# Two-layer hybrid block: low parts of the split weights written over the raw pieces, four slots instead of four and two

## The reference

```python
def first_block(x, ...):
    for layer in range(2):
        x = x + 0.5 * swiglu(rmsnorm(x, ffn1_norm[layer]), ffn1_w_gu[layer], ffn1_w_down[layer])
        h = rmsnorm(x, mix_norm[layer])
        y = mixer_gated_deltanet(h, ...) if layer == 0 else mixer_sliding_window_sinks(h, ...)
        x = x + y
        x = x + 0.5 * swiglu(rmsnorm(x, ffn2_norm[layer]), ffn2_w_gu[layer], ffn2_w_down[layer])
    return rmsnorm(x, final_norm)

def second_block(x, p, ...):                      # hybrid, ffn4 and ple in the kernel's names
    z = rms_norm(x, norm_mix) @ w_in              # q, k, v; RWKV columns; two gates
    attn = windowed_gqa(q, k, v, sink)            # 8 query heads of 64, 2 key heads, T = 256
    rwkv = rwkv7_time_mix(shifted z, ...)         # 8 heads of 64, both directions
    x = x + merged(gates, attn @ w_up_attn, rwkv @ w_up_rwkv) @ w_out
    x = x + squared_relu_ffn(rms_norm(x, ...))    # width 4096
    return x + gated per-layer embedding of p
```

## Time and profile before

| | |
|---|---|
| median of 3 runs | 1692.92 us (1690.53 to 1695.64) |
| the profiled execution | 1697.04 us, span 1695.0 us |
| mean granted TensorE clock | 0.974 of full speed |
| matmuls on PE | 15411 |
| splits of whole pieces on ACT and DVE | 223 each; the two permuted pieces are split in 8 quarters |

### The profile page before, as it was taken

The page is one execution under the profiler, slowest core; times in us unless marked ns, Lnnn a source line. Parts: engine busy times, 40 slices in busy tenths (PEclk is TensorE's granted clock), DMA queues, the critical chain, the costliest instruction groups (busy, mean ns, idle before and its releaser), DMA issues.

```text
span 1695.0 us, 35795 instructions
## 1 busy us (share of the span) xinstructions
PE 1592.7 (94%) x15411; PEld 1527.7 (90%) x15411; DVE 1055.6 (62%) x1274; ACT 730.1 (43%) x811; POOL 74.9 (4%) x53
## 2 busy tenths in 40 slices
PE   7999899878899999999998999999978999999997
PEld 7999899777899999999988999999857778999997
DVE  4765577653666647664677665568666654767345
ACT  5343345532534345433555433454643322555342
POOL 1000000000100001000101000031110000100000
PEclk9999999989999999999999999999979999999998
DMA  8655545000656556555434665554100021555550
GB/s 274 209 187 186 191 134 173 26 2 19 203 177 190 182 186 187 179 192 191 158 101 150 185 192 194 184 183 142 58 2 3 2 101 52 173 176 183 188 191 34
DMA packets 155064, 243.24 MB, mean 144 GB/s; under 512 B 9283, under 2 KB 106174, under 8 KB 154814
## 3 DMA queue, kind: packets, MB, share of 16 engines
q1 hardware_dynamic: 154510, 240.63, 43.6%
q10 hardware_dynamic: 432, 0.79, 0.2%
HBM read 240.34 MB, written 1.05 MB: 142 GB/s over the span
## 4 chain that ended last, share of the span: by engine, by line
PE 83%; DVE 10%; ACT 4%; issue 2%; DMA 0%; SPq 0%; DVEq 0%; ACTq 0%
PE dense_ps L2390 23%; PE dense_ps L2391 22%; PE dense_ps L2392 22%; PE mixer_ps L456 3%; DVE w_lo L2770 2%; PE dense_ps L456 2%; ACT w_hi L2595 1%; PE mixer_ps L1082 1%; PE mixer_ps L1657 1%; DVE qkv L887 1%; PE mixer_ps L1091 1%; DVE xT L2886 1%; ACT ly_r L502 0%; PE mixer_ps L1100 0%; DMA raw<-in_ffn_w_gu 0%
## 5 line engine op out<-in xcount | busy, mean ns | idle before, releaser
L2770 DVE TENSOR_TENSOR w_lo<-raw,w_hi 128x2048 fp32r<-128x2048 f32 x223 | 513.1, 2301 | 377.1 <-ACT w_hi L2595 376.5
L2390 PE MATMUL dense_ps<-h_hi,w_hi 128*128 128x256 f32 x2368 | 669.8, 283 | 24.4 <-DVE h_lo L2845 15.1
L2391 PE MATMUL dense_ps<-h_lo,w_hi 128*128 128x256 f32 x2368 | 663.3, 280 | 0.0
L2392 PE MATMUL dense_ps<-h_hi,w_lo 128*128 128x256 f32 x2368 | 663.3, 280 | 0.0
L2595 ACT ACTIVATE w_hi<-raw 128x2048 fp32r<-128x2048 f32 x223 | 427.6, 1918 | 513.1 <-PE dense_ps L2392 490.6
L2390 PEld LDWEIGHTS dense_ps<-h_hi,w_hi 128*128 128x128 f32 x2368 | 451.0, 190 | 31.6 <-issue 27.3
L2392 PEld LDWEIGHTS dense_ps<-h_hi,w_lo 128*128 128x128 f32 x2368 | 449.3, 190 | 0.0
L2391 PEld LDWEIGHTS dense_ps<-h_lo,w_hi 128*128 128x128 f32 x2368 | 447.7, 189 | 0.7 <-issue 0.5
L2390 PE MATMUL dense_ps<-g_hi,w_hi 128*128 128x256 f32 x960 | 266.5, 278 | 2.8 <-DVE w_lo L2770 2.6
L2392 PE MATMUL dense_ps<-g_hi,w_lo 128*128 128x256 f32 x960 | 266.0, 277 | 0.0
L2391 PE MATMUL dense_ps<-g_lo,w_hi 128*128 128x256 f32 x960 | 266.0, 277 | 0.0
(11 more groups left out here) (526 smaller groups left out, 1858.9 us busy)
## 6 DMA issues: line engine op xcount, KB each, us to landing
raw<-in_ffn_w_gu SPq DMA_DIRECT2D x176, 512.0 KB, 4.7
raw<-in_ffn_w_down SPq DMA_DIRECT2D x88, 512.0 KB, 4.2
raw<-in_w_ff SPq DMA_DIRECT2D x64, 512.0 KB, 4.3
raw<-in_w_in SPq DMA_DIRECT2D x36, 512.0 KB, 4.2
raw<-in_a_w_in SPq DMA_DIRECT2D x32, 512.0 KB, 4.4
raw<-in_a_w_out SPq DMA_DIRECT2D x8, 512.0 KB, 4.1
raw<-in_b_w_in SPq DMA_DIRECT2D x8, 512.0 KB, 4.0
raw<-in_b_w_out SPq DMA_DIRECT2D x8, 512.0 KB, 4.1
```

Of the source, the lines that this page charges most:

```text
L2390: pe.matmul(o, hi, mh, start=start, stop=False)
L2391: pe.matmul(o, hi, ml, start=False, stop=False)
L2392: return pe.matmul(o, lo, mh, start=False, stop=stop)
L2770: dve.tensor_tensor(w_lo[:, p % 2, :], raw[:, p % RAW_SLOTS, :], w_hi[:, p % 2, :].bitcast(F32), ALU.subtract).then_inc(lo_ready, 1)
```

## The change

- **Slots.** There is one number of slots, four, for `w_hi` and for `raw`; `w_lo` has the memory of `raw`, so DVE writes the low part over the raw piece. The load of piece p now waits for `piece_used` of piece p - 4. ACT's split waits for the load alone.
- **Order of splits.** ACT's first split of the next stage stands ahead of its wait for `dense_drained` in `norm`; DVE's is at the end of the down projection (`pieces_of[down] - 1`), and the one in `residual` behind the first half is gone. In mixer_a one split moves into the second inverse (level 3 on ACT, level 5 on DVE) and two follow the last output. In mixer_b the splits at the beginning go, and two stand together at the end (n == 6 on ACT, n == 7 on DVE). In the hybrid's norm two stand where one stood, and out2's last `splits(2)` becomes 3.
- **Hybrid heads.** Query columns are no longer permuted: the pieces of in2 are split like all others. The queries of a key head lie on both partition halves, so the keys are needed on both: a matmul with the constant `swap` writes them to a sixth column block of `qk`. `scores(0)` moves from tile 1 to tile 3, `turned_(0)` from 6 to 7, `values(0)` to tile 1 of chunk 1.
- **Shared space.** mixer_a's second group lies over slot 0 of `w_hi`, slot 0 of `raw` and the end of the arena (`h_lo`); the hybrid's matrices over slots 2 and 3 of `w_hi` and of `raw`. POOL waits for `piece_used` before it fills them.

```diff
-RAW_SLOTS = 4
-SPLIT_SLOTS = 2
+SLOTS = 4
...
-    raw = fixed.take("raw", [P, RAW_SLOTS, PIECE])
-    w_hi = fixed.take("w_hi", [P, SPLIT_SLOTS, PIECE], F32R)
-    w_lo = fixed.take("w_lo", [P, SPLIT_SLOTS, PIECE], F32R)
+    w_hi = fixed.take("w_hi", [P, SLOTS, PIECE], F32R)
+    raw_at = fixed.at
+    raw = fixed.take("raw", [P, SLOTS, PIECE])
+    w_lo = Map(nc, raw_at, fixed.at).take("w_lo", [P, SLOTS, PIECE], F32R)
...
-    HEAD_PIECES = [PIECE_OF["in2"] + i for i in range(2)]
-
-    def by_heads(tensor, slot, k):
-        return tensor[:, slot, 512 * k:512 * k + 512].rearrange("p (s t d) -> p t s d", s=2, t=4)
...
-    SET_A = (group_set(m, 0), group_set(Map(nc, base, base + 3 * PIECE * 4), 1))
...
+    assert (PIECE_OF["a_out"] + 3) % SLOTS == 0
+    SET_A = (group_set((m, m, m), 0),
+             group_set([Map(nc, at_, at_ + PIECE * 4) for at_ in (base, raw_at, arena - PIECE * 4)], 1))
...
+            if lv == 3:
+                splits(1)
...
-        pool.wait_ge(lo_ready, PIECE_OF["a_out"] + 2)
+        pool.wait_ge(piece_used, PIECE_OF["a_out"])
...
+            if lv == 5:
+                splits(1)
...
-        splits(1)
         finished(1)
-        splits(1)
+        splits(2)
...
             if n in (4, 6):
-                splits(1)
-        splits(1)
+                splits(1 + n // 6)
...
             if n in (5, 7):
-                splits(1)
+                splits(1 + n // 7)
...
-    m = Map(nc, base, base + RAW_SLOTS * PIECE * 4)
-    assert PIECE_OF["up_attn"] % RAW_SLOTS == 0
+    m = Map(nc, base + 2 * PIECE * 4, raw_at)
...
-                 "slots": (0, 1, 2, 3), "ot": 2 * s_, "sink": 32 + 4 * s_} for b in range(NB) for s_ in range(2)]
+                 "slots": (0, 2, 1, 3), "ot": 2 * s_, "sink": 32 + 4 * s_} for b in range(NB) for s_ in range(2)]
 
     def q_c(g, t):
-        return qk[64 * g["half"]:64 * g["half"] + 64, t, P * g["blk"]:P * g["blk"] + P]
+        return qk[64 * (t % 2):64 * (t % 2) + 64, 2 * g["half"] + t // 2, P * g["blk"]:P * g["blk"] + P]
 
     def k_c(g, t):
-        return qk[64 * g["half"]:64 * g["half"] + 64, 4, :]
+        return qk[64 * (t % 2):64 * (t % 2) + 64, 4 if t % 2 == g["half"] else 5, :]
...
+            if n == 0 and kt == 1:
+                pe.wait_ge(c_qkv, 1)
+                pe.matmul(M_ps[:, 3, T:2 * T], constant("swap"), qk[:, 4, :], start=True, stop=True).then_inc(c_vturn, 1)
+            if 1 <= n <= 4 and kt == (1 if n == 1 else 0):
+                values(n - 1)
+            if 0 <= n < 4 and kt == (1 if n else 3):
                 if n == 0:
-                    pe.wait_ge(c_qkv, 1)
+                    pe.wait_ge(c_qkv, 2)
                     pe.wait_ge(att_mask, masks_c["at"])
                 scores(n)
-            if 0 <= n < 4 and kt == 6:
+            if 0 <= n < 4 and kt == (6 if n else 7):
                 if n:
                     pe.wait_ge(att_out, base_ + n)
                 turned_(n)
-            if 1 <= n <= 4 and kt == 0:
-                values(n - 1)
...
-        pool.wait_ge(lo_ready, PIECE_OF["up_attn"])
+        pool.wait_ge(piece_used, PIECE_OF["in2"] + 2 * COUNT_OF["in2"])
...
+        dve.wait_ge(c_vturn, 2)
+        dve.tensor_copy(qk[:, 5, :], M_ps[:, 3, T:2 * T]).then_inc(c_qkv, 1)
...
-        splits(2)
+        splits(3)
...
-                slot = p % RAW_SLOTS
-                if p >= RAW_SLOTS:
-                    sp.wait_ge(lo_ready, p - RAW_SLOTS + 1 + RAW_SLOTS * turn)
+                slot = p % SLOTS
+                if p >= SLOTS:
+                    sp.wait_ge(piece_used, p - SLOTS + 1 + SLOTS * turn)
...
-                act.wait_ge(raw_loaded[p % RAW_SLOTS],
-                            32 * (p // RAW_SLOTS + 1 + turn) + (16 if p >= PIECE_OF["b_in"] else 0))
-                if p >= SPLIT_SLOTS:
-                    act.wait_ge(piece_used, p - SPLIT_SLOTS + 1 + 4 * turn)
-                if p in HEAD_PIECES:
-                    assert isinstance(turn, int)
-                    for k in range(4):
-                        last = act.activation(as_heads(w_hi, p % 2, k), by_heads(raw, p % RAW_SLOTS, k), ACT.Copy)
-                    last.then_inc(hi_ready, 1)
-                    return
-                act.activation(w_hi[:, p % 2, :], raw[:, p % RAW_SLOTS, :], ACT.Copy).then_inc(hi_ready, 1)
+                act.wait_ge(raw_loaded[p % SLOTS],
+                            32 * (p // SLOTS + 1 + turn) + (16 if p >= PIECE_OF["b_in"] else 0))
+                act.activation(w_hi[:, p % SLOTS, :], raw[:, p % SLOTS, :], ACT.Copy).then_inc(hi_ready, 1)
...
                 for half in range(2):
+                    if half == 0 and stage in BEFORE:
+                        splits(1)
...
-                    if half == 0 and stage in BEFORE or stage == "ffn0" and half == 0:
+                    if half == 0 and stage == "ffn0":
...
-                    splits(1 if stage in ("mixer_b", "hybrid") else 2)
+                    splits(2)
...
-                dve.tensor_tensor(w_lo[:, p % 2, :], raw[:, p % RAW_SLOTS, :], w_hi[:, p % 2, :].bitcast(F32),
+                dve.tensor_tensor(w_lo[:, p % SLOTS, :], raw[:, p % SLOTS, :], w_hi[:, p % SLOTS, :].bitcast(F32),
...
-                    if e == 0 and ahead_of_split:
-                        splits(1)
...
-                        splits(pieces_of[down] - 2)
-                    residual(down, 1.0 if up == "ff1" else 0.5, s != "ffn0")
+                        splits(pieces_of[down] - 1)
+                    residual(down, 1.0 if up == "ff1" else 0.5)
```

More of the change, by code:

```diff
@@ L272, in alone @@
         eng.nop().then_inc(sem("passed"), 1)
-    raw_loaded = [sem(f"raw_loaded{i}") for i in range(RAW_SLOTS)]
+    raw_loaded = [sem(f"raw_loaded{i}") for i in range(SLOTS)]
     hi_ready = sem("hi_ready")
@@ L386, in build, with group_set @@
     m.at = at
-    def group_set(m_, g):
-        return {n: m_.take(f"{n}{g}", [P, c, P]) for n, c in (
-            ("v_tok", 8), ("neg_lt", 8), ("att_t", 8), ("q_dec", HG), ("k_dec", HG), ("inv", 8), ("inv_t", 8))}
-    SET_A = (group_set(m, 0), group_set(Map(nc, base, base + 3 * PIECE * 4), 1))
+    PARTS = ((("v_tok", 8), ("neg_lt", 8)), (("att_t", 8), ("q_dec", HG), ("k_dec", HG)), (("inv", 8), ("inv_t", 8)))
+    def group_set(maps, g):
+        return {n: m_.take(f"{n}{g}", [P, c, P]) for m_, part in zip(maps, PARTS) for n, c in part}
+    assert (PIECE_OF["a_out"] + 3) % SLOTS == 0
+    SET_A = (group_set((m, m, m), 0),
+             group_set([Map(nc, at_, at_ + PIECE * 4) for at_ in (base, raw_at, arena - PIECE * 4)], 1))
     at = m.at
@@ L1027, in beside_first @@
                 query_norm(1)
-                dve.wait_ge(lo_ready, PIECE_OF["a_out"] + 2)
+                dve.wait_ge(piece_used, PIECE_OF["a_out"])
                 values_kept(1)
@@ L1138, in sink @@
             of_heads = bcast[:, g["sink"]:g["sink"] + 4]
-            if g["slots"][1] == 1:
-                return of_heads.rearrange("p (a b) -> p a b", b=2)
             return of_heads.rearrange("p (a b) -> p b a", b=2)
@@ L1345, in mixer_b_dve @@
             last.then_inc(dense_drained, 1)
-            splits(1)
+            if e:
+                splits(1)
             if "ffn3" in STAGES:
@@ L1366, in build @@
     zp = m.take("zp", [P, ZT, T + 2])
-    qk = m.take("qk", [P, 5, T])
+    qk = m.take("qk", [P, 6, T])
     v_c = m.take("v_c", [P, 1, T])
@@ L1396, in build @@
     ar_raw = m.take("ar_raw", [P, 2, NB, 2, P])
-    m.at = base + 2 * PIECE * 4
+    m = Map(nc, raw_at + 2 * PIECE * 4, raw_at + 4 * PIECE * 4)
     gram_raw = m.take("gram_raw", [P, 8, 4 * P])
@@ L1777, in hybrid_act @@
         act.wait_ge(dense_drained, 2 + f0 + 2)
-        act.activation(sq[:, 0:5, :], qk[:, :, :], ACT.Square).then_inc(c_sq, 1)
+        act.activation(sq[:, 0:5, :], qk[:, 0:5, :], ACT.Square).then_inc(c_sq, 1)
         splits(1)
@@ L2468, in wide @@
                         w0 = 1024 * k + P * nt
-                        last = three(o, w_hi[:, p % 2, w0:w0 + P], w_lo[:, p % 2, w0:w0 + P],
+                        last = three(o, w_hi[:, p % SLOTS, w0:w0 + P], w_lo[:, p % SLOTS, w0:w0 + P],
                                      mh[:, kt, :], ml[:, kt, :],
@@ L2763, in split_lo @@
                 dve.wait_ge(hi_ready, p + 1 + 4 * turn)
-                if p in HEAD_PIECES:
-                    for k in range(4):
-                        last = dve.tensor_tensor(as_heads(w_lo, p % 2, k), by_heads(raw, p % RAW_SLOTS, k),
-                                                 as_heads(w_hi, p % 2, k).bitcast(F32), ALU.subtract)
-                    last.then_inc(lo_ready, 1)
-                    return
-                dve.tensor_tensor(w_lo[:, p % 2, :], raw[:, p % RAW_SLOTS, :], w_hi[:, p % 2, :].bitcast(F32),
+                dve.tensor_tensor(w_lo[:, p % SLOTS, :], raw[:, p % SLOTS, :], w_hi[:, p % SLOTS, :].bitcast(F32),
                                   ALU.subtract).then_inc(lo_ready, 1)
@@ L2877, in next_stage, with residual @@
```

(4 more changed lines are left out.)

15 lines of the change are left out of this document (5 added, 10 removed).

## The result

| | before | changed kernel |
|---|---|---|
| median of the first set | 1691.0 us (5 executions) | 1678.27 us (1670.65 to 1679.05) |
| ratio, 95% interval | | 0.9914 (0.9895 to 0.9933) |
| second set | 1696.87 us | 1678.52 us, ratio 0.9896 (0.9857 to 0.9935) |
| third set | 1689.78 us | 1680.26 us, ratio 0.9936 (0.9909 to 0.9963) |
| profiled execution | 1697.04 us | 1678.34 us, span 1676.3 us |

A set is a group of kernels that were run together with the kernel before. The kernel became about 15 us faster (16.3, 17.1 and 11.4 us between the means of the three sets); the prediction said 12.7 and 1680.

The account below looks back on a forecast made before the run. TensorE (PE), busy 1592.7 of 1695.0 us, was taken as the bound. Gains of 7.3 + 4.7 + 2.65 less 1.9 made 12.7 us, giving 1680 us on the scale of the median; eight-in-ten range 1672 to 1688.

Parts of the forecast that it names:

- Feeding PE: Dense stretches: loads start three pieces (16.2 us) ahead and need about 9.4 us with splits, 6.8 us spare; pace kept.
- rival C: Dense stretches: loads landing more than 6.8 us late stop PE, making the kernel slower, 1703 us; chance 0.05.
- Stage changes: Six stage changes: splitting the next first piece before `xT` starts `h_lo` 1.18 us sooner (hybrid 1.39); gain 7.3 us.
- rival A: Stage changes: the second half comes late, POOL folds slowing `h_lo`, and eats the gain; 7 us left, 1686; chance 0.15.
- Waits for `w_lo`: PE's waits in in2, ple, a_in, for `mg_lo` and before mixer_a shrink, 4.7 us; ff2's and ple_gate's long waits stay.
- leave the clock as it is: The two waits that stay, in ff2 and ple_gate, are still followed by a granted clock near its 1.2 GHz level.
- Hybrid heads: Hybrid: scores across both partition halves save 3.6 us of PE, less 0.45 for a swap matmul and 0.5 stall; net 2.65.
- What costs: Moved splits cost 0.8 us in mixer_a's inverse, 0.8 in b_out, 0.3 in the hybrid's norm; POOL's clearing hidden; sum 1.9.
- rival D: Larger gain: the splits' lead also removes the remaining stalls and the 1.2 GHz clock behind them; 21 us, 1672; chance 0.09.

Follow-up runs that it names:

- ends_ahead: Changed kernel with splits also ahead of each up projection's last body, ahead of ple's root and behind mixer_b's last attention output: 1671.42 us; run again, 1679.94 us.
- heads_only: Kernel before with only the hybrid heads as changed (no permutation, keys swapped by one matmul, first scores two tiles later): 1696.0 us, ratio 1.0005.
- hybrid_lead: Changed kernel with in2's splits one piece further ahead, one more before the first softmax and one less behind the last: 1678.83 us, ratio 0.9932.
- order_only: Kernel before with its old slots (four raw, two split) and only the new order of splits at stage changes, on ACT and DVE: 1713.31 us, ratio 1.0104.
- dve_order: Kernel before with its two split slots and only DVE's part of the new order; ACT's splits stay where they stood: 1693.5 us, ratio 1.001.
- changes_undone: Changed kernel, four slots kept, with the old split order at stage changes: 1692.02 us, ratio 0.9983; run again, 1684.7 us, ratio 0.9967.

## Why the prediction was right, and where it was not

- **Feeding PE.** Right. Loads now bound ACT, never PE; rival C did not come.
- **Stage changes**, 7.3 us: measured 6.9, each wait 0.51 to 0.63 us (0.95 ahead of ffn3, where `xT` is made in four short operations). The second half cost nothing, so rival A is out: `h_lo` operations of 1.53 us beside a fold on POOL are still there (627.67 at the change to ffn2), but behind the pair that PE needs. The prediction's reason, that the split stands between `xT` and `h_lo`, held. That order and slots are both needed was not in it; it would have been right to ask what two slots with the new order do.
- **Waits for `w_lo`**, 4.7 us: measured 4.6, and the two waits of 2.4 us stood as said. That they "leave the clock as it is" did not hold in the profiled execution: the clock stayed at 1.00 behind both. The reason given for their length, order on DVE, was shown by ends_ahead.
- **Hybrid heads**, 2.65 us: the step that failed. It read 3.6 us off PE as time and put what DVE and ACT would make PE wait in return at 0.5 us, for the first softmax alone. Measured: 3.4 us off the scores, and 0.7 us off in2, with 2.1 us of new waits and a swap in it. The bound of the stretch was DVE with ACT, as heads_only and hybrid_lead showed.
- **What costs**, 1.9 us: measured 1.1. b_out 0.63 for 0.8 (ends_ahead gives it back), the inverse 0.5 for 0.8, the hybrid's norm nothing. POOL's clearing ran from 1214.2 to 1226.2, ahead of DVE's first use at 1232.8, hidden as said. Whether the 1.0 us of the serial stretch behind in2 belongs here is open.
- **The sum.** Waits came to 11.0 instead of 12.7. The clock added 4.6 us in the second set and 1.9 in the third, a term that the forecast put at nothing and only rival D had. Two errors of 2 and of 2 to 5 us partly cancelled: that 1680 stands so close to 1678.27 is partly luck, and its reasons account for three quarters of the gain.

## What to carry to other kernels

Slots and order are one resource: moving a split ahead of a wait pays only if its buffer is free by then, and with too few buffers the early operation waits at the head of its queue and holds back what the next stage needs. Time taken off the busiest engine in a stretch counts only if that engine is what the stretch waits for; look at the length of the other engines' chain per group first. And where executions of one kernel differ by more than the edit, count its waits in the trace, and run kernels that are to be compared in one set.

## What the runs showed of the hardware

PE runs the 48 dense matmuls of a piece (128 x 128 by 256 columns, first start to last) in 5.33 or in 5.53 us, at a granted clock of 1.00 and with the same instructions. The pace holds for whole jobs and changes mostly where the run of dense matmuls is broken: at waits, some as short as 0.04 us (576.95 in the kernel before), and without a wait where four to six matmuls of the sum of squares stand between two pieces (457.05 there). The same kernel shows it in other stages in another execution. It weighs 5 to 24 us in the executions profiled (22 to 116 pieces of 0.205).

Behind the same wait the granted clock falls or does not. For the wait of 2.2 to 2.4 us in ff2 it fell in the kernel before, order_only, dve_order and both profiles of changes_undone, and stayed at 1.00 in heads_only, hybrid_lead and in all three of the changed kernel; where it fell it was at its lower level for about 3.4 us. It fell in five of the six profiles of kernels that wait 1.5 us or more at most stage changes, and in none of the four others; ten profiles do not show whether that is more than chance. It fell behind a shorter wait too, 1.89 us at the change to mixer_b in dve_order, and not behind the 2.1 us at the change to ffn2 in the same trace.
